# Seven block products in place of eight in 16 weight slabs of a decoder layer's last projection

## What is computed

```python
        x = _layer_norm(DEEPNORM_ALPHA * x + mix, ln1_gain[l], ln1_bias[l])
        h = jnp.square(jax.nn.relu(x @ w_ff1[l])) @ w_ff2[l]
        x = _layer_norm(DEEPNORM_ALPHA * x + h, ln2_gain[l], ln2_bias[l])
```

## Time and profile before

| what | value |
|---|---|
| device time, median of 3 runs | 1253.62 us (1252.44 to 1254.64) |
| span of the profiled execution (no time of its own is given beside it) | 1251.5 us |
| TensorE matmul busy | 1233.0 us, 99% |
| TensorE weight loads busy | 1040.4 us, 83% |
| VectorE busy | 758.5 us, 61% |
| ScalarE busy | 584.4 us, 47% |
| share of the chain that ended last, by engine | TensorE 56%, VectorE 1% |
| last projection, first matmul to last slab pair | about 885.9 to 1236 us |

### The profile page before, as it was taken

How to read it: one execution, slowest core, us unless ns; L and a number is a source line. 1 busy time by engine, 2 the same in 40 slices (tenths; PEclk the granted TensorE clock), 3 DMA queues, 4 the chain that set the end, 5 groups by cost and what they waited for, 6 DMA issues and landing times.

```text
span 1251.5 us, 23267 instructions
## 1 busy us (share of the span) xinstructions
PE 1233.0 (99%) x9636; PEld 1040.4 (83%) x9636; DVE 758.5 (61%) x808; ACT 584.4 (47%) x638; POOL 75.6 (6%) x43
## 2 busy tenths in 40 slices
PE   8999999999999999999999999999999999999997
PEld 8888888888788778888888888888888888888885
DVE  5688887565766376755554554545645555755557
ACT  6754545555756244444434334343444444444442
POOL 0022111000000000164000000000000000000000
PEclk9999999999999999999999999999999999999999
DMA  9455565343431256545555555555665555555541
GB/s 336 153 203 171 174 245 187 104 136 107 165 102 54 89 203 234 213 139 198 182 187 199 174 197 187 181 201 175 215 241 182 195 201 184 189 198 196 183 158 67
DMA packets 34194, 222.21 MB, mean 178 GB/s; under 512 B 4717, under 2 KB 5101, under 8 KB 8782
## 3 DMA queue, kind: packets, MB, share of 16 engines
q1 hardware_dynamic: 34126, 221.21, 51.2%
HBM read 219.10 MB, written 2.10 MB: 177 GB/s over the span
## 4 chain that ended last, share of the span: by engine, by line
PE 56%; DVE 1%; ACT 0%; issue 0%; DVEq 0%
PE ps L503 56%; DVE stats L2046 0%; DVE xres L2045 0%; DVE xres L2182 0%; DVE xres L2180 0%; DVE xres L2170 0%; ACT xres L1219 0%; DVE xres L2174 0%; DVE moments L2049 0%; PE ps L1148 0%; DVE moments L2056 0%; ACT moments L1219 0%; DVE shift_diag L2196 0%; DVE moments L2055 0%; DVEq L2039 0%
## 5 line engine op out<-in xcount | busy, mean ns | idle before, releaser
L1622 DVE TENSOR_TENSOR wlo<-stage,whi 128x2048 fp32r<-128x2048 f32 x183 | 426.1, 2328 | 374.3 <-ACT whi L1219 373.5
L1219 ACT ACTIVATE whi<-stage 128x2048 fp32r<-128x2048 f32 (+1 forms) x196 | 370.0, 1889 | 487.6 <-PE ps L503 482.8
L503 PE MATMUL ps<-acts,whi 128*128 128x512 f32 (+1 forms) x1728 | 535.0, 392 | 3.0 <-DVE wlo L1649 1.7
L503 PEld LDWEIGHTS ps<-acts,wlo 128*128 128x128 f32 x1680 | 315.8, 188 | 72.5
L503 PE MATMUL ps<-acts,wlo 128*128 128x256 f32 x1680 | 334.7, 278 | 0.0
L503 PEld LDWEIGHTS ps<-acts,whi 128*128 128x128 f32 x1728 | 263.9, 189 | 7.6 <-issue 2.0
L503 PE MATMUL ps<-whi,shi 128*128 128x512 f32 x504 | 138.2, 392 | 0.1
L503 PE MATMUL ps<-whi,slo 128*128 128x512 f32 x504 | 136.9, 390 | 0.0
L503 PE MATMUL ps<-wlo,shi 128*128 128x512 f32 x504 | 136.8, 389 | 0.0
L503 PEld LDWEIGHTS ps<-whi,shi 128*128 128x128 f32 x504 | 92.7, 188 | 23.1 <-issue 4.4
L503 PEld LDWEIGHTS ps<-whi,slo 128*128 128x128 f32 x504 | 94.6, 188 | 20.2
(11 more groups left out here) (251 smaller groups left out, 991.6 us busy)
## 6 DMA issues: line engine op xcount, KB each, us to landing
stage<-w_ff SPq DMA_DIRECT2D x128, 1024.0 KB, 5.0
stage<-w_in SPq DMA_DIRECT2D x48, 1024.0 KB, 5.0
stage<-w_out SPq DMA_DIRECT2D x16, 1024.0 KB, 5.0
stage<-w_in SPq DMA_DIRECT2D x6, 512.0 KB, 9.3
xstage<-xT SPq DMA_DIRECT2D x4, 512.0 KB, 7.2
TM_TT<-eyes SPq DMA_DIRECT2D x4, 512.0 KB, 7.8
xres<-x SPq DMA_DIRECT2D x1, 2048.0 KB, 9.6
gain<-ln_gain SPq DMA_DIRECT2D x2, 1024.0 KB, 7.8
```

Source lines behind the costliest of these rows:

```text
L503: return pe.matmul(out, lhsT, rhs, start=start, stop=stop, skip_group_check=True)
L1219: return act.activation(out, in_, func, **kw)
L1622: TTn(wlo[k0 % NHL][:, :], stage[k0 % NST][:, :], f(whi[k0 % NHL][:, :]), ALU.subtract).then_inc(s_lo, 1)
```

## The change

In 16 slabs, `QUADS` = 4, 7, ..., 28 of the first sweep and 38, 41, ..., 56 of the second, the eight block products become the seven of Strassen's scheme (in Winograd's form). For such a slab VectorE forms four sums of weight blocks (`tsum`, 128 x 4 x 512) and four sums of activation blocks (`asum`, 128 x 4 x 128), in six instructions (`quad_sums`); they stand two slabs ahead, after the split of slab n-2. ScalarE rounds both (`thi`, `ashi`; `quad_sums_hi`), VectorE takes both remainders (`tlo`, `aslo`; `quad_sums_lo`). Of the slab itself only three of the four blocks are rounded and have a remainder taken (`hi_own`, `lo_own`, 1536 columns). TensorE then makes 21 matmuls (`quad`). Three of the seven products go straight into a bank of the sweep, four into "shared" banks: those that otherwise lie unused in that sweep. After the last such slab of a sweep VectorE adds the shared banks to `xres` in three pieces (`shared_taken`, in the turns of slabs 29 to 31 and 57 to 59), after one copy by ScalarE (`shared_copied`); slab 32 waits for that. The factor `ALPHA` moves from `add_and_measure` to `shared_taken`. All hardware loops of the last projection are written out on TensorE, ScalarE and VectorE. Some semaphores elsewhere are merged (left out below), and the host stores two blocks of those 16 slabs in the other order.

```diff
+QUADS = (tuple(range(4, 29, 3)), tuple(range(38, 57, 3)))
+QUAD = QUADS[0] + QUADS[1]
...
+        tsum = at("tsum", 12, [P, 4, 512])
+        thi, tlo = at("thi", 10, [P, 4, 512], F32R), at("tlo", 11, [P, 4, 512], F32R)
...
+            def quad(n):
...
+                pe.wait_ge(s_hi, g + 1)
+                own = ((shared[0], plain[0, 0], whole[1], first), (direct[0, 0], plain[0, 1], whole[2], False))
+                for acc, x, y, start in own:
+                    for part in range(2):
+                        highs(acc, x, y, start, part)
+                pe.wait_ge(s_lo, g + 1)
+                for acc, x, y, start in own:
+                    lows(acc, x, y, end and start)
+                pe.wait_ge(s_ql, 2 * k + 2)
+                for part in range(2):
+                    highs(direct[0, 1], summed[3], whole[3], False, part)
+                lows(direct[0, 1], summed[3], whole[3], False)
+                mixed = ((shared[1], summed[1], added[0], first), (shared[2], summed[0], added[1], first),
+                         (shared[3], summed[2], added[2], first), (direct[1, 0], plain[1, 1], added[3], False))
+                for part in range(2):
+                    for acc, x, y, start in mixed:
+                        highs(acc, x, y, start, part)
+                for acc, x, y, start in mixed:
+                    last = lows(acc, x, y, end and start)
+                last.then_inc(s_used, 1)
...
+                pe.wait_ge(s_ahi, n + 1)
+                pe.wait_ge(s_alo, n + 1)
+                if n in QUAD:
+                    quad(n)
...
+            def hi_own(g):
...
+                act.wait_ge(s_used, g - 1)
+                A(whi[g % NHL][:, 512:SLAB], stage[g % NST][:, 512:SLAB], ACT.Copy).then_inc(s_hi, 1)
...
+            def quad_sums_hi(n):
...
+                    act.wait_ge(s_used, G_FF2 + QUAD[k - 1] + 1)
+                act.wait_ge(s_qs, 6 * k + 5)
+                A(thi[:, :, :], tsum[:, :, :], ACT.Copy).then_inc(s_qh, 1)
+                act.wait_ge(s_qs, 6 * k + 6)
+                A(ashi[:, :, :], asum[:, :, :], ACT.Copy).then_inc(s_qh, 1)
...
-                link(STT(x, x, ALPHA, ps[:, 4 * a + (q + 2) % 4 if n else out_bank(a, q), :], ALU.mult, ALU.add))
+                if n:
+                    link(TTn(x, x, ps[:, direct_bank(h, a, q % 2), :], ALU.add))
...
+            def quad_sums(n):
...
+                dve.wait_ge(s_stage[g % NST], 16 * (g // NST + 1))
+                TTn(tsum[:, 0:2, :], src[:, 1::2, :], src[:, 0:1, :].broadcast_to([P, 2, 512]), ALU.add).then_inc(s_qs, 1)
+                TTn(asum[:, 0:2, :], x[:, 1:2, :].broadcast_to([P, 2, P]), x[:, 0::3, :], ALU.subtract).then_inc(s_qs, 1)
+                dve.wait_ge(s_qs, 6 * k + 1)
+                TTn(tsum[:, 2, :], tsum[:, 0, :], src[:, 3, :], ALU.add).then_inc(s_qs, 1)
+                dve.wait_ge(s_qs, 6 * k + 2)
+                TTn(asum[:, 2, :], x[:, 0, :], asum[:, 1, :], ALU.subtract).then_inc(s_qs, 1)
+                dve.wait_ge(s_qs, 6 * k + 3)
+                TTn(tsum[:, 3, :], tsum[:, 2, :], src[:, 2, :], ALU.add).then_inc(s_qs, 1)
+                dve.wait_ge(s_qs, 6 * k + 4)
+                TTn(asum[:, 3, :], x[:, 2, :], asum[:, 2, :], ALU.subtract).then_inc(s_qs, 1)
...
+            for n in range(1, LAST_PAIR + 2):
+                g, after = G_FF2 + n, n - QUADS[sweep(n)][-1]
+                if n in QUAD:
+                    quad_sums_lo(n)
+                    lo_own(g)
...
+                else:
+                    lo(g, g)
+                split(pair_of_hidden(n), n, n % 2, g - 1)
+                if n + 2 in QUAD:
+                    quad_sums(n + 2)
+                if 1 <= after < 4:
+                    shared_taken(sweep(n), after - 1)
+                if 1 <= n - DFF // P // 2 < 5:
+                    add_and_measure(1, *FIRST_SWEEP[n - DFF // P // 2 - 1])
```

More of the change, by code:

```diff
@@ L369, in build, with sweep, direct_bank, shared_bank @@
         SHIFT = (2, 3, 6)
+        def sweep(n):
+            return n // (DFF // P // 2)
+        def direct_bank(h, a, q):
+            return 4 * a + 2 - 2 * h + q
+        def shared_bank(h, i):
+            return 4 * (i // 2) + 2 * h + i % 2
+        def quad_no(n):
+            return QUAD.index(n)
+        def quads_to(h):
+            return len(QUADS[0]) + h * len(QUADS[1])
+        def rounded_count(n, i):
+            return 2 * quad_no(n) + sweep(n) + i
         def out_bank(a, q):
@@ L1169, in _, with highs, lows @@
                     pairs(ff1_bank(k), i * 4 + (G_FF1 + 2 * k), G_FF1 + 2 * k)
[L1171 to L1188, removed]
+            def quad(n):
+                g, h, b, k = G_FF2 + n, sweep(n), n % 2, quad_no(n)
+                w, first, end = g % NHL, n == QUADS[h][0], n == QUADS[h][-1]
+                plain = {(a, kk): (shi[b][:, kk, tok(a)], slo[b][:, kk, tok(a)]) for a in range(TT_) for kk in range(2)}
+                summed = [(ashi[:, i, :], aslo[:, i, :]) for i in range(4)]
+                whole = [(whi[w][:, 512 * j:512 * j + 512], wlo[w][:, 512 * j:512 * j + 512]) for j in range(4)]
+                added = [(thi[:, i, :], tlo[:, i, :]) for i in range(4)]
+                shared = [ps[:, shared_bank(h, i), :] for i in range(4)]
+                direct = {(a, q): ps[:, direct_bank(h, a, q), :] for a in range(TT_) for q in range(2)}
+                def highs(acc, x, y, start, part):
+                    mm(acc, x[part], y[0], start=start and part == 0, stop=False)
+                def lows(acc, x, y, stop):
+                    return mm(acc, x[0], y[1], start=False, stop=stop)
+                pe.wait_ge(s_hi, g + 1)
[18 more added lines that the diff above has]
+                last.then_inc(s_used, 1)
@@ new lines, in _ @@
+            for n in range(LAST_PAIR):
+                h, local = sweep(n), n % (DFF // P // 2)
+                if local == 0:
+                    pe.wait_ge(s_sum, N_FF1 - 1 + h)
+                    if h:
+                        pe.wait_ge(s_pd, 8)
+                if n in QUAD and n == QUADS[h][0]:
+                    if h:
+                        pe.wait_ge(s_lnk, 16)
+                    else:
+                        pe.wait_ge(s_sum, N_FF1)
+                pe.wait_ge(s_ahi, n + 1)
+                pe.wait_ge(s_alo, n + 1)
+                if n in QUAD:
+                    quad(n)
+                else:
+                    end = n == DFF // P // 2 - 1
+                    rows(G_FF2 + n, G_FF2 + n, n, h, local == 0, end, each=end)
@@ L2136, in _ @@
                 ff1(N_FF1 // 2 - 1, k, k == 1)
[L2137 to L2148, removed]
-                    dve.wait_ge(s_lnp, 8)
-                if 1 <= n - 2 * NG < 5:
-                    add_and_measure(1, *FIRST_SWEEP[n - 2 * NG - 1])
@@ L2152, in _, with lo_own @@
[L2152 to L2159, removed]
+            def lo_own(g):
+                dve.wait_ge(s_hi, g + 1)
+                TTn(wlo[g % NHL][:, 512:SLAB], stage[g % NST][:, 512:SLAB], f(whi[g % NHL][:, 512:SLAB]), ALU.subtract
+                    ).then_inc(s_lo, 1)
@@ new lines, in quad_sums_lo, with shared_taken @@
+            def quad_sums_lo(n):
+                k = quad_no(n)
+                if k:
+                    dve.wait_ge(s_used, G_FF2 + QUAD[k - 1] + 1)
+                dve.wait_ge(s_qh, rounded_count(n, 1))
+                TTn(tlo[:, :, :], tsum[:, :, :], f(thi[:, :, :]), ALU.subtract).then_inc(s_ql, 1)
+                dve.wait_ge(s_qh, rounded_count(n, 2))
+                TTn(aslo[:, :, :], asum[:, :, :], f(ashi[:, :, :]), ALU.subtract).then_inc(s_ql, 1)
+            def shared_taken(h, part):
+                top, right, bottom, corner = (xres[:, a, quarter(2 * h + q)] for a, q in ((0, 0), (0, 1), (1, 0), (1, 1)))
+                copied, v, z = (tsum[:, i, :] for i in range(3))
+                p1, p5, p7, p6 = (ps[:, shared_bank(h, i), :] for i in range(4))
+                if part == 0:
+                    dve.wait_ge(s_ql, 2 * quads_to(h))
+                    dve.wait_ge(s_used, G_FF2 + QUADS[h][-1] + 1)
+                    dve.wait_ge(s_qh, 2 * quads_to(h) + h + 1)
+                    STT(top, top, ALPHA, p1, ALU.mult, ALU.add).then_inc(s_pd, 1)
+                    TTn(v, p6, copied, ALU.subtract).then_inc(s_pd, 1)
+                    dve.wait_ge(s_pd, 8 * h + 2)
+                    TTn(z, p7, v, ALU.add).then_inc(s_pd, 1)
+                elif part == 1:
+                    STT(right, right, ALPHA, v, ALU.mult, ALU.add).then_inc(s_pd, 1)
+                    dve.wait_ge(s_pd, 8 * h + 3)
+                    STT(corner, corner, ALPHA, z, ALU.mult, ALU.add).then_inc(s_pd, 1)
+                    dve.wait_ge(s_pd, 8 * h + 4)
+                    TTn(right, right, p5, ALU.add).then_inc(s_pd, 1)
+                else:
+                    dve.wait_ge(s_pd, 8 * h + 5)
+                    TTn(corner, corner, p5, ALU.add).then_inc(s_pd, 1)
+                    STT(bottom, bottom, ALPHA, z, ALU.mult, ALU.subtract).then_inc(s_pd, 1)
```

(12 more changed lines are left out.)

89 lines of the change are left out of this document (54 added, 35 removed).

## The result

The changed kernel takes **1259.18 us** (median of 5 runs, 1257.92 to 1260.73) against 1253.44 us for the kernel before beside it (5 runs, 1252.44 to 1254.64). The ratio is **1.0046, 95% interval 1.0036 to 1.0057**: slower by 4.5 to 7.1 us. The forecast was 1255.4 us, within 0.2% and on the slow side. The time lies in its range of 1248 to 1263 and on the side it leaned to, but past the 0.2%: of the +5.7 us only +1.8 were foreseen.

The account below looks back on a forecast made before the run. TensorE was taken to bound the stage, with a second bound, the chain readying the next slab, 0.4 us below. Terms -1.9 + 2.4 - 0.4 + 0.2 + 1.5 = +1.8 gave 1255.4 us; range 1248 to 1263.

Parts of the forecast that it names:

- loops written out: Last projection, slabs 2 to 62: 60 slabs at 5.449 us instead of 5.481, -1.9 us.
- first sums: Sums in slab 2's turn: the next slab can start 5.63 us after it, against 5.45, +0.2 us.
- 13 periods: Full periods of three slabs, one with seven products: +0.17 us each; the prediction counted 14, +2.4 us.
- slabs 37 to 41 with slab 38's period: In slab 36's turn, slab 38's sums meet the last `add_and_measure`: 6.95 us against 5.45, +1.5, plus one period's +0.17.
- last such slab of each sweep: Last seven-product slab of each sweep has no sums behind it: 2 x -0.22 = -0.4 us.
- the period: Three slabs from a seven-product slab on: 16.52 us against 3 x 5.449 = 16.35, +0.17 us.
- the edge: Slab 36's turn, where slab 38's sums meet the last `add_and_measure`: 6.95 us against 5.45, +1.5 us.
- Rival 1: VectorE's instructions don't overlap at the joints from `slo` through the sums to `wlo`: 1269 us if all seven; chance 0.25.
- the rival's mild form: Only two of the seven VectorE joints lack overlap: +3.8 us, 1259 us; chance 0.17.
- Rival 2: VectorE has more room than counted, so only the two-buffer chain counts: 1248.2 us, or 1246.6 with a shorter restart; chance 0.22.
- Rival 3: The full saving of the removed matmuls arrives, 10.9 us besides the loops' 1.9: 1240.8 us; chance 0.03.

Follow-up runs that it names:

- sums_tiny: The change with the six sums of every seven-product slab but the first cut to one column; 1253.15 us, 0.9990 of the kernel before.
- sums_longer: The change with one more sum of 512 columns in front of the six; 1269.82 us, 1.0134 of the kernel before.
- three_buffers: The change with a third pair of `whi` and `wlo` buffers in slabs 2 to 56, GpSimd's multiplications behind slab 63; 1243.28 us, 0.9923 of before.
- unrolled_only: The kernel before with the last projection's loops written out, all 64 slabs with eight products; 1254.82 us, 0.9996 of before.
- pool_late: The change with GpSimd's two multiplications held back from slab 37's turn to slab 60's; 1258.87 us, 1.0038 of the kernel before.
- sums_early: The change with the six sums for slab n+3 one turn earlier, behind `slo` of slab n; 1254.48 us, 1.0014 of the kernel before.

## Why the prediction was right in kind and short in size

**The mechanism.** It was right. A seven-product slab is followed after 5.29 us, not 4.76 (forecast 5.23); slab n+2 waits for VectorE's `slo` behind the six sums (0.45 us of standing, forecast 0.39); more is given back than saved. sums_tiny and sums_longer show the sums as the cause of the second standing, three_buffers shows the two buffers as the cause of what remains.

**The sum, term by term.** Measured are `whi` starts in the change's trace over 5.449 us a slab, the prediction's base:

| term | forecast us | measured us |
|---|---|---|
| loops written out (before: 328.87 against 60 x 5.449) | -1.9 | -1.9; unrolled_only -2.1 |
| first sums, slabs 2 to 4 | +0.2 | +0.28; in unrolled_only, without sums, +0.27 |
| 13 periods (slabs 5 to 28, 42 to 56) | 13 x 0.17 = +2.2 | 2.35 + 1.48 = **+3.8** |
| slabs 37 to 41 with slab 38's period | 1.5 + 0.17 = +1.7 | **+2.87** |
| last such slab of each sweep, three and four turns | -0.4 | -0.31 |
| elsewhere (slabs 32 to 36, and 0.28 from `whi` of slab 61 to slab 62, whose cause stays open) | 0 | +0.35 |
| sum | +1.8 | +5.1 |

**First miss: the period.** It was summed to 16.52 and is 16.64. The parts are in the rows: `whi` starts 0.26 us behind the slab (943.28 to 943.54) and not 0.20, which was read in a turn of the hardware loop; the sums take 951.46 - 948.38 = 3.08 and not 3.05; differences of 0.01 to 0.02 at the two starts and in the last slab make up the rest. 0.12 us is little in one period, and 1.6 in 13 of them. Half of it is a price that was read in one form of the code and carried into the other, although before shows the right one too: in its own written-out slabs 60 to 62 `whi` starts 0.26 us behind the slab.

**Second miss: the edge.** The step said that slab 36's turn meets `add_and_measure`, and stopped there. That part holds: in sums_tiny the `whi` interval from slab 38 is 5.44 us where the change has 7.08. With GpSimd away, pool_late's intervals from slab 37 to slab 42 are 5.44, 7.04, 4.76, 6.00 and 5.87, together 1.9 over 5 x 5.449, where 1.7 was forecast. The other 1.0 of the change's 2.87 is GpSimd's two multiplications, which the prediction named nowhere: it asked which engines wait for VectorE, not which other engine used its idle time.

**What held.** `thi` (951.35 to 953.27) is hidden, as was forecast. `shared_taken` costs nothing that can be seen here (slabs 57 to 60 are together 0.13 us under the base). `tlo`, `aslo`, the shorter `wlo` and `slo` are hidden too (`slo` ends at 959.34, the next seven-product slab starts at 959.92).

**The rivals.** Rival 1, no overlap of VectorE's instructions, fell: each of the sums starts 0.07 to 0.09 us ahead of the recorded end of the one in front (`slo` ends at 948.38, the first sum starts at 948.30; the last ends at 951.46, `wlo` starts at 951.38). The Trainium skill, "VectorE: DVE Perf Modes", section "The DRAIN you can't avoid", says that the next instruction does not start until the pipe is empty, and adds that one that is not held back starts earlier; these rows show the second, which the prediction's sentence on that section left out. The result lies where the rival's mild form did (1259), by another cause. Rival 2, VectorE with room to spare, is what sums_early makes true, with 16.2 us a period where the rival had 3 x 5.449 - 0.22 = 16.13; it is not what the change does. Rival 3, the full saving, needed a third buffer, and then came nearly whole.

**The chance.** With 0.40 for no change and 0.35 for slower the wrong one of two neighbours was ahead. That the range held the time is in part luck: it reached past the 0.2% up to 1263 only for the mild form of rival 1, which fell. The forecast itself said that each 0.1 us on VectorE's chain is 1.6 us, which from +0.14% leads past 0.2%. An error of 0.1 us in a chain of ten terms was to be expected, and both things left out, GpSimd and the later `whi`, were costs.

## What to carry to other kernels

Work taken off the busiest engine is worth no more than the slack of the chain that feeds it. Here 0.68 us were saved in a slab, but the next one can follow only 5.29 us after its start where 5.44 was the pace, so 0.15 us is left. The remedy was one more buffer, worth nothing alone and 9.6 us with the saving. Added work belongs into a turn where the engine idles, and before placing it, look which other engine (here GpSimd) uses that idle time. Where a small term is multiplied by dozens of slabs, read its price in the form of the code that will run.

## What was not expected of the hardware

**GpSimd and VectorE take turns.** In the rows at 1093 us VectorE's `tlo` keeps its 2.29 us while GpSimd, released at the same time, gets on late; then `aslo` is 1.10 us longer and `wlo` 1.09, while GpSimd's two instructions take 2.36 longer (4.91 against 2.55). Less its usual 0.68 us, `aslo` (recorded end 1097.36) would begin at 1096.68, 1.0 us after `tlo` ends (1095.67), and one GpSimd instruction took 2.55 / 2 = 1.3 before. This looks like alternating, each waiting for a whole instruction of the other, rather than both running at a slower pace; the trace shows the two GpSimd instructions only as one row, so the turns are inferred. The Trainium skill, "SBUF — State Buffer", section "SBUF: two separate sides", says so: the two share a pair of ports, and a GpSimd instruction and a VectorE one with two SBUF inputs lock each other out for an instruction's length. The lengths in the trace agree, and pool_late shows the price at this place, 1.1 us.

**ScalarE wakes later in written-out code.** `whi` starts 0.26 us after the slab's first matmul here and in unrolled_only (0.25 to 0.28), and before 0.20 in ScalarE's loop but 0.26 in its written-out slabs 60 to 62. Why stays open.
